# Moving the room of h to the front of SBUF in a two-layer fp32r kernel on one core

## The reference

```python
x = first_block(...)    # mod = silu(c) @ ada_w; h = rms_norm(x) * (1 + scale) + shift
                        # proj = h @ w_in  (9296 columns); sparse attention and a gated
                        # recurrence on the parts of proj; x += gate * (mix @ w_out)
x = second_block(...)   # proj = rms_norm(x) @ w_in_2 (8704 columns); a long convolution and
                        # attention on the parts; merged = g_h*(y_h @ w_br_hyena)
                        #   + g_a*(y_a @ w_br_attn); x += merged @ w_out_2
                        # x += (silu(h2 @ w_ffn_gate) * (h2 @ w_ffn_up)) @ w_ffn_down
```

## The kernel before

| tensor | first byte | modulo 1024 | modulo 64 |
|---|---|---|---|
| x_res | 16,512 | 128 | 0 |
| raw, raw_lo | 32,896 | 128 | 0 |
| w_hi | 85,280 | 288 | 32 |
| w_lo | 101,664 | 288 | 32 |
| h_hi | 118,048 | 288 | 32 |
| h_lo | 134,432 | 288 | 32 |
| hbuf, proj, proj2, hid_hi | 150,816 | 288 | 32 |
| hid_lo | 183,584 | 288 | 32 |

## Time and profile before

### The profile page before, as it was taken

The page is one execution under the profiler, slowest core; times in us unless marked ns, Lnnn a source line. Parts: engine busy times, 40 slices in busy tenths (PEclk is TensorE's granted clock), DMA queues, the critical chain, the costliest instruction groups (busy, mean ns, idle before and its releaser), DMA issues.

```text
span 2333.9 us, 23790 instructions
## 1 busy us (share of the span) xinstructions
PE 2138.9 (92%) x9261; PEld 1678.1 (72%) x9261; DVE 1439.1 (62%) x2254; ACT 884.3 (38%) x1070; POOL 21.5 (1%) x13
## 2 busy tenths in 40 slices
PE   6799999997597989999996779898999999999999
PEld 1278888886465867788784458786888888878887
DVE  4478654667846977787687766646545545444443
ACT  1134433444423443344440053344444444443333
POOL 0000000000300000000000000000000000000000
PEclk9889998998767989999997899998999999999999
DMA  9948755553002647566562005454555555555554
GB/s 348 377 163 291 268 193 164 185 194 135 1 1 76 218 135 223 179 214 203 189 207 77 1 10 190 151 191 133 191 193 185 192 187 190 190 179 192 189 197 162
DMA packets 208223, 406.34 MB, mean 174 GB/s; under 512 B 10809, under 2 KB 16369, under 8 KB 207729
## 3 DMA queue, kind: packets, MB, share of 16 engines
q1 hardware_dynamic: 203232, 397.24, 51.4%
q10 hardware_dynamic: 4882, 7.62, 1.0%
HBM read 402.74 MB, written 2.10 MB: 173 GB/s over the span
## 4 chain that ended last, share of the span: by engine, by line
PE 80%; DVE 11%; DMA 5%; ACT 2%; issue 1%; SPq 0%; DVEq 0%; ACTq 0%
PE ps L376 74%; PE pm L446 5%; DMA raw<-in_ada_w 3%; DVE raw_lo L354 1%; DMA raw<-in_w_in 1%; DVE mod_part L994 1%; DVE sc_i L1101 1%; DVE w_lo L354 1%; PE pm L730 0%; PE pm L458 0%; DVE xtmp L1344 0%; ACT w_hi L340 0%; DVE xtmp L1345 0%; DVE xtmp L1346 0%; DMA decay<-in_decay 0%
## 5 line engine op out<-in xcount | busy, mean ns | idle before, releaser
L340 ACT ACTIVATE w_hi<-raw 128x1024 fp32r<-128x1024 f32 x648 | 678.9, 1051 | 988.9 <-PE ps L376 942.9
L376 PE MATMUL ps<-w_hi,h_hi 128*128 128x512 f32 (+1 forms) x2336 | 929.7, 398 | 35.9 <-DVE h_lo L809 19.1
L376 PE MATMUL ps<-w_hi,h_lo 128*128 128x512 f32 (+1 forms) x2336 | 916.3, 392 | 0.0
L354 DVE TENSOR_TENSOR w_lo<-raw,w_hi 128x1024 fp32r<-128x1024 f32 x328 | 400.9, 1225 | 420.5 <-ACT w_hi L340 417.9
L376 PEld LDWEIGHTS ps<-w_hi,h_hi 128*128 128x128 f32 x2336 | 445.9, 191 | 133.3 <-DVE h_lo L809 21.6
L354 DVE TENSOR_TENSOR raw_lo<-raw,w_hi 128x1024 fp32r<-128x1024 f32 (+1 forms) x320 | 384.0, 1202 | 223.3 <-ACT w_hi L340 218.6
L376 PEld LDWEIGHTS ps<-w_hi,h_lo 128*128 128x128 f32 x2336 | 446.1, 191 | 101.7
L376 PE MATMUL ps<-raw_lo,h_hi 128*128 128x512 f32 (+1 forms) x1280 | 506.2, 395 | 0.0
L376 PE MATMUL ps<-w_lo,h_hi 128*128 128x512 f32 x1056 | 413.3, 391 | 0.0
L376 PEld LDWEIGHTS ps<-raw_lo,h_hi 128*128 128x128 f32 x1280 | 245.3, 192 | 52.1 <-issue 0.2
L376 PEld LDWEIGHTS ps<-w_lo,h_hi 128*128 128x128 f32 x1056 | 200.0, 189 | 41.0
(11 more groups left out here) (294 smaller groups left out, 1334.5 us busy)
## 6 DMA issues: line engine op xcount, KB each, us to landing
raw<-in_w_in SPq DMA_DIRECT2D x140, 1024.0 KB, 5.2
raw<-in_w_ffn_gate SPq DMA_DIRECT2D x44, 1024.0 KB, 5.1
raw<-in_w_ffn_up SPq DMA_DIRECT2D x44, 1024.0 KB, 5.2
raw<-in_w_ffn_down SPq DMA_DIRECT2D x44, 1024.0 KB, 5.1
raw<-in_ada_w SPq DMA_DIRECT2D x32, 1024.0 KB, 7.5
raw<-in_w_out SPq DMA_DIRECT2D x32, 1024.0 KB, 5.1
proj<-in_ada_w SPq DMA_DIRECT2D x16, 1024.0 KB, 9.4
raw<-in_w_br_hyena SPq DMA_DIRECT2D x8, 1024.0 KB, 5.1
```

The costliest lines, as they stand in the source:

```text
L340: nc.scalar.activation(w_hi[:, p % HRING, :, 0:gm.width], raw[:, k % RING, e:e + HT, 0:gm.width], ACT.Copy).then_inc(hi_done, 1)
L354: nc.vector.tensor_tensor(low_half(gm, p), raw[:, k % RING, e:e + HT, 0:gm.width], w_hi[:, p % HRING, :, 0:gm.width].bitcast(F32), ALU.sub ...
L376: mm = nc.tensor.matmul(ps[pair][:, t, 0:gm.width], l[:, tok], r[:, i, 0:gm.width], start=(k == 0 and q == 0), stop=(k == kt - 1 and q == 2))
```

## The change

The allocation of `h_room`, with all the tensors that share it, moves from behind `ring_room` to the very front of what the kernel allocates. No instruction, wait, transfer or size changes. With the sizes above, the first bytes become:

| tensor | before | after | after, modulo 1024 | after, modulo 64 |
|---|---|---|---|---|
| h_hi | 118,048 | 16,512 | 128 | 0 |
| h_lo | 134,432 | 32,896 | 128 | 0 |
| x_res | 16,512 | 49,280 | 128 | 0 |
| raw, raw_lo | 32,896 | 65,664 | 128 | 0 |
| small tensors | from 65,664 | from 98,432 | 128 | 0 |
| w_hi | 85,280 | 118,048 | 288 | 32 |
| w_lo | 101,664 | 134,432 | 288 | 32 |
| hbuf, proj, proj2, hid_hi | 150,816 | 150,816 | 288 | 32 |

```diff
@@ build(), ahead of x_res
+        st = ExitStack()
+        h_hi = sb("h_hi", [P, KT, SEQ], F32R, st)
+        h_lo = sb("h_lo", [P, KT, SEQ], F32R, st)
+        st.close()
...
+        h_room = ctx.enter_context(nc.sbuf_tensor("h_room", [P, 2 * KT * SEQ], F32))
 
         x_res = sb("x_res", [P, TT, D])
@@ build(), behind ring_room
         ring_end = ctx.enter_context(nc.sbuf_tensor("ring_room", [P, 2 * HRING * HT * GW], F32))
 
-        st = ExitStack()
-        h_hi = sb("h_hi", [P, KT, SEQ], F32R, st)
-        h_lo = sb("h_lo", [P, KT, SEQ], F32R, st)
-        st.close()
...
-        h_room = ctx.enter_context(nc.sbuf_tensor("h_room", [P, 2 * KT * SEQ], F32))
 
         st = ExitStack()
         sb("hbuf_below", [P, TT, D], F32, st)
```

More of the change, by code:

```diff
@@ L123, in sb @@
             return stack.enter_context(nc.sbuf_tensor(name, shape, dt))
+        st = ExitStack()
+        h_hi = sb("h_hi", [P, KT, SEQ], F32R, st)
+        h_lo = sb("h_lo", [P, KT, SEQ], F32R, st)
+        st.close()
+        st = ExitStack()
+        mod_row = sb("mod_row", [P, 2 * D], F32, st)
+        mod_part = sb("mod_part", [P, 2, GW], F32, st)
+        st.close()
+        st = ExitStack()
+        qT = sb("qT", [P, NH, SEQ], F32, st)
+        kT = sb("kT", [P, NH, SEQ], F32, st)
+        qiT = sb("qiT", [P, IDX_H // 2, SEQ], F32, st)
+        kiT = sb("kiT", [P, SEQ], F32, st)
+        lb_tmp = sb("lb_tmp", [P, A_W], F32, st)
+        st.close()
+        st = ExitStack()
+        lf = sb("lf", [P, TT, A_W], F32, st)
+        kc = sb("kc", [P, TT, A_W], F32, st)
+        qa = sb("qa", [P, TT, A_W], F32, st)
+        ka = sb("ka", [P, TT, A_W], F32, st)
+        st.close()
+        st = ExitStack()
+        sb("decay_below", [P, 2 * HY], F32, st)
+        decay = sb("decay", [P, TT, HY], F32, st)
+        hf = sb("hf", [P, TT, HY], F32, st)
+        hb = sb("hb", [P, TT, HY], F32, st)
+        st.close()
+        st = ExitStack()
+        x0T = sb("x0T", [P, 8, SEQ], F32, st)
+        zT = sb("zT", [P, 8, SEQ], F32, st)
+        z_tok = sb("z_tok", [P, TT, HY], F32, st)
+        st.close()
+        h_room = ctx.enter_context(nc.sbuf_tensor("h_room", [P, 2 * KT * SEQ], F32))
         x_res = sb("x_res", [P, TT, D])
```

## The result

The changed kernel is slower: 2344.81 us against 2333.65 us (medians of 19 executions each), a ratio of 1.0081 with a 95% interval of 1.0057 to 1.0105. The range held the time, but I had forecast no change, and this one is clear of noise. The profiled execution took 2345.36 us, its span 2343.6 us.

The account below looks back on a forecast made before the run. TensorE was taken to bound the kernel, line 376's matmuls holding 74% of the chain. Every term was put at 0, so the forecast stayed at 2335 us, with an 8-in-10 range from 2305 to 2397.

Parts of the forecast that it names:

- The bound: Whole kernel: TensorE busy 92% of the span, matmuls of line 376 holding 74% of the chain; feeders have room.
- TensorE, stationary operands: Matmuls of line 376 with h moved: unknown, bounded from 16.5 us gained to 58.3 us lost, taken as 0.
- the 13.2 ns a triple that `raw_lo` pays: Line 376 before the change: three matmuls cost 693.4 ns with `raw_lo` as low half, 680.2 ns with `w_lo`.
- phase conflict: Line 376, `w_lo` products: operands differing modulo 64 cost 13.2 ns; 58.3 us lost, 2395 us; chance 0.20.
- The page on two ports: TensorE reads its two operands through independent ports, so no placement matters: 0; some 215.8 ns between matmuls.
- The boundary of 64 KB: Crossing it within a triple costs 13.2 ns: `raw_lo` gains up to 16.5 us, `w_lo` loses up to 17.3; chance 0.12.
- the whole extra gone: Line 376: h and ring no longer neighbours, 512 columns cost 213.3 ns; 109 us gained, 2227 us; chance 0.06.
- The late loads: Second input projection: three late loads (8.61, 11.65, 8.10 us) come from small loads on the same queue and stay.
- The clock: If all rows stand and the time still moves over 1%, it came from the clock or the late loads.

Follow-up runs that it names:

- m1: Kernel without the network, only groups of 48 fp32r matmuls on TensorE at varied start addresses: 10.89 us a group level modulo 256, 11.24 us at 96 apart.
- e2: First kernel with a 32-byte pad ahead of the room of h and one behind it: 2345.94 us, ratio 1.0072.
- e6: Changed kernel with one pad of 96 bytes ahead of the ring, all rooms at 128 modulo 256: 2316.1 us, ratio 0.9946.
- e1: Changed kernel with a 32-byte pad ahead of the room of h and one behind it: 2352.94 us, ratio 1.0102.
- e3: First kernel with one pad of 32 bytes ahead of the ring: 2337.24 us, ratio 1.0018.
- m2: Matmul-only kernel as m1, with other start addresses and operand shapes: 10.91 us a group for level starts from +32 to +224.

## Why the prediction was wrong

**The bound** was read rightly. Line 376 paced the kernel, the feeders had room, and 1225 ns of VectorE stayed.

**The step that failed** is "TensorE, stationary operands ... I take 0". The chain pieces and m1 show 7.5 ns on each of 3168 matmuls and 1.1 ns on 3744, 27.9 us. I had the right row in hand, the 13.2 ns a triple that `raw_lo` pays. I set it aside because hid and h agreed at different distances. But they agreed in phase as well (all stood at 32 modulo 256): rows that agree in the suspected quantity can't acquit it. They only cleared distance, and m1, e2 and e6 confirm that distance and front cost nothing.

**The rival "phase conflict"** had the right mechanism, at a chance of 0.20, with two errors. The modulus is 256, not 64; e1, e2 and e3 showed that. The argument that I set against it, that a fixed phase need not matter, had no row behind it. And its price was too high: 58.3 us, for I charged a `w_lo` matmul 13.2 ns, the whole excess of a `raw_lo` triple, where it took 7.5. The mark I had set for it was met (a `w_lo` matmul with h over 230 ns), and 46 us for 192 matmuls was foreseen where 44.98 came. A mixed triple is no sum of its members: by m1's figures two level pairs and one 32 apart would average 229.0 ns, and the measured group (L81) takes 231.5; with the low half of the stationary operand as the odd one (L89) it takes 11.19 us, 233.1 ns, as much as all three apart. Why is open.

**The page on two ports**, "TensorE: Matmul & The Clock Gate" of the Trainium skill, pointed to 0. m1 shows TensorE alone, with nothing else running, at 226.9 or 234.2 ns by the start of its stationary operand only; the measurement decides, and against the page's rule as I applied it. Its 2.5 ns above the columns fit plain float32 if the columns are counted twice: the starts of recorded matmuls of 512 columns stand 429 ns apart, which is twice 213.3 plus 2.5. They do not fit fp32r, with 13.4 ns.

**The boundary of 64 KB** and **the whole extra gone** fell: hid's pairs stayed at 389 ns though the ring now crosses such a boundary, and no fp32r product went below 226.7 ns.

**The late loads** did not stay as they were: the chain after has two of them (11.56 and 8.11 us) where three stood. That stretch came out 1.4 us shorter, as said with the chain.

**The clock.** I named it only as a last resort. It hid two thirds of the loss in the profiled execution, 18.5 of 27.9 us, and in the medians 11 us are left of 28 to 31. So it is luck that the time came within 10 us of my 2335; the changed kernel's two executions at 2359 and 2365 have the mean clock of a slow recurrence. Why the changed kernel meets the quick recurrence in most runs and the first one in fewer than half was not tried.

## What to carry to other kernels

In a stream of fp32r matmuls of this shape (128x128 by 128x512) that is bound by TensorE, put the first bytes of moving and stationary operands level modulo 256, at a multiple of 32, and do so for every member of the product; here 96 bytes of padding gave 0.6%, and a careless move of a room cost 0.8% (1.2% by the paces, 1.3% with the recurrence kept warm). For other shapes time both: none of the four others tried in m2 was cheaper level. Divide pieces of the chain by their count before and after: 7.5 ns on a matmul show where medians with two heaps do not. And where two rows acquit a cause, ask first in what else they agree.

## What the runs showed of the hardware

An fp32r matmul of 128x128 with 128x512 took 226.7 ns at best at the full clock, 13.4 ns above its columns, and 229 to 234.3 ns where the start addresses differed by other multiples of 32 modulo 256 (m1, with no other engine at work). Starts that are not multiples of 32 cost up to 11.41 us / 48 = 237.7 ns even when level. In the first kernel's recurrence TensorE was busy 46.66 of 47 us at a granted clock of 0.53, so being recorded busy with small matmuls did not bring the full clock. In other executions the same 256 matmuls took 28.32 us at 1.00.
